# Stick-breaking attention on one core: the weights' transposes moved from TensorE to VectorE's 32x32 blocks and sixteen small copies

## The reference

```
z         = q @ k.T * HEAD_DIM ** -0.5          # 12 heads x 64, causal
earlier   = k_pos < q_pos
log_beta  = log_sigmoid(z)
log_keep  = where(earlier, log_sigmoid(-z), 0)
log_later = cumsum(log_keep, reverse) - log_keep
weights   = where(earlier, exp(log_beta + log_later), 0)
o_A       = weights @ v
...
o = concat(o_A * silu(g_A), o_B * silu(g_B), o_C * silu(g_C)) @ w_out
```

## Time and profile before

| what | value |
|---|---|
| median of 3 runs | 2174.82 us (2173.72 to 2175.7) |
| the profiled execution | 2172.31 us, span 2170.6 us |
| TensorE matmuls, busy | 2112.1 us (97%) |
| VectorE, busy | 1016.4 us (47%) |
| ScalarE, busy | 735.1 us (34%) |
| granted TensorE clock, mean | 0.993 |

### The profile page before, as it was taken

How to read it: one execution, slowest core, us unless ns; L and a number is a source line. 1 busy time by engine, 2 the same in 40 slices (tenths; PEclk the granted TensorE clock), 3 DMA queues, 4 the chain that set the end, 5 groups by cost and what they waited for, 6 DMA issues and landing times.

```text
span 2170.6 us, 31985 instructions
## 1 busy us (share of the span) xinstructions
PE 2112.1 (97%) x13712; PEld 1909.9 (88%) x13712; DVE 1016.4 (47%) x1947; ACT 735.1 (34%) x1280; POOL 9.4 (0%) x28
## 2 busy tenths in 40 slices
PE   5999999999999999999999999999999999999996
PEld 4998988889888898999999999999999978888885
DVE  7446565656656565433334342444334563334224
ACT  6234343443434343322223232333223453222221
POOL 0000000000000000000000000000000000000000
PEclk8999999999999999999999999999999999999998
DMA  6321312222121222213131222222222352336423
GB/s 239 76 71 45 78 37 64 64 55 74 45 65 50 65 65 44 80 40 85 40 84 40 65 64 56 60 54 54 52 66 51 120 172 98 101 105 241 135 83 126
DMA packets 320678, 174.16 MB, mean 80 GB/s; under 512 B 170440, under 2 KB 295128, under 8 KB 318776
## 3 DMA queue, kind: packets, MB, share of 16 engines
q1 hardware_dynamic: 319368, 164.12, 27.2%
q0 software_dynamic: 1168, 7.99, 0.9%
HBM read 139.21 MB, written 36.06 MB: 81 GB/s over the span
## 4 chain that ended last, share of the span: by engine, by line
PE 89%; DVE 7%; ACT 2%; DMA 1%; issue 0%; SPq 0%; DVEq 0%; ACTq 0%
PE ps L792 19%; PE ps L793 18%; PE ps L794 18%; PE ps L989 6%; PE ps L988 6%; PE ps L987 6%; PE ps L877 3%; PE ps L971 3%; PE ps L844 3%; PE ps L942 3%; PE ps L904 2%; PE ps L889 2%; DVE arena L1380 2%; DVE arena L1374 1%; DVE arena L1388 1%; ACT arena L1171 1%
## 5 line engine op out<-in xcount | busy, mean ns | idle before, releaser
L792 PE MATMUL ps<-act_hi,w_hi 128*128 128x352 f32 x2688 | 887.1, 330 | 9.8 <-DVE arena L1315 5.8
L793 PE MATMUL ps<-act_lo,w_hi 128*128 128x352 f32 x2688 | 870.1, 324 | 0.0
L794 PE MATMUL ps<-act_hi,w_lo 128*128 128x352 f32 x2688 | 870.0, 324 | 0.0
L792 PEld LDWEIGHTS ps<-act_hi,w_hi 128*128 128x128 f32 x2688 | 507.5, 189 | 41.5 <-issue 28.6
L793 PEld LDWEIGHTS ps<-act_lo,w_hi 128*128 128x128 f32 x2688 | 507.9, 189 | 0.0
L794 PEld LDWEIGHTS ps<-act_hi,w_lo 128*128 128x128 f32 x2688 | 507.6, 189 | 0.0
L1291 DVE TENSOR_TENSOR w_lo<-w_raw,w_hi 128x512 fp32r<-128x512 f32 x352 | 240.5, 684 | 321.9 <-ACT w_hi L1149 243.8
L987 PE MATMUL ps<-w_hi,act_hi 128*128 128x512 f32 x576 | 226.5, 393 | 5.4 <-DVE w_lo L1291 3.0
L989 PE MATMUL ps<-w_hi,act_lo 128*128 128x512 f32 x576 | 229.0, 398 | 0.0
L988 PE MATMUL ps<-w_lo,act_hi 128*128 128x512 f32 x576 | 228.1, 396 | 0.0
L1073 ACT ACTIVATE w_hi<-w_raw 128x512 fp32r<-128x512 f32 x224 | 138.9, 623 | 143.0 <-DMA w_raw<-in_w_in_dram 143.0
(11 more groups left out here) (122 smaller groups left out, 1684.2 us busy)
## 6 DMA issues: line engine op xcount, KB each, us to landing
w_raw<-in_w_in_dram SPq DMA_DIRECT2D x176, 256.0 KB, 2.9
w_raw<-in_w_out_dram SPq DMA_DIRECT2D x128, 256.0 KB, 3.0
w_raw<-in_w_in_dram SPq DMA_DIRECT2D x96, 128.0 KB, 2.5
arena<-in_x_prompt_dram SPq DMA_DIRECT2D x8, 1024.0 KB, 6.0
out_dram<-arena SPq DMA_DIRECT2D x14, 512.0 KB, 2.8
value_scratch<-arena SPq DMA_DIRECT2D x48, 132.0 KB, 3.4
arena<-value_scratch SPq DMA_DIRECT2D x12, 512.0 KB, 4.2
mixed_scratch<-arena SPq DMA_DIRECT2D x10, 528.0 KB, 4.0
```

The source lines that it names most:

```text
L792: mm(bank(g, GN), wh, ah, start=(k == 0), stop=False)
L793: mm(bank(g, GN), wh, al, start=False, stop=False)
L794: last = mm(bank(g, GN), wl, ah, start=False, stop=(k == KT - 1))
```

## The change

For steps 0 to 8 of A (`by_blocks`) `stick_turn` is gone from TensorE. In its place VectorE turns the whole tile of 128x1024 in blocks of 32x32 into a new buffer `turned` (1024 columns of the arena), and sixteen copies bring block (i, j) of each 128x128 square back to place (j, i) in `stick`: each copy moves 32 partitions x 8 blocks of 32 columns. ScalarE does nine, VectorE seven. The values wait for both (`wt_act`, `wt_dve`). A score set of banks is free once the subtraction has read it (`t_ready`). The sample's step keeps its five small transposes and its copies. `FLIGHT` is 2, so the number of `stick` buffers is as before, and the expression of `gate_at` gives the same ticks as before. The values of the last unit's last two steps are planned 0.2 ticks later. The cached keys, values and the work area lie 96 columns lower in the arena.

```diff
+FLIGHT = 2
+def by_blocks(u, i):
+    return UNITS[u][0] == "a" and A_STEPS[i][0][0] < TT
...
-        return START[u][n] + 7
+        return START[u][n] + 7.2
...
# pe_plan
-            plan += [(START[u][i], "scores", u, i), (turn_at(u, i), "turn", u, i)]
+            plan.append((START[u][i], "scores", u, i))
+            if not by_blocks(u, i):
+                plan.append((turn_at(u, i), "turn", u, i))
# act_plan
+            if by_blocks(u, i):
+                plan.append((s + 5.3, "place_weights", u, i))
+            else:
+                plan.append((w + (0.25 * pace(u, i) if kind == "b" else 0.5), "turned", u, i))
# dve_plan
+                if by_blocks(u, i):
+                    plan += [(s + 4.75, "turn_weights", u, i), (s + 4.76, "place_weights", u, i)]
...
+        stick = [work[:, 1024 * i:1024 * i + 1024] for i in range(FLIGHT)]
+        turned = work[:, 2048:3072]
...
+        def block_of(ap, q, n):
+            return ap[32 * q:32 * q + 32, :].rearrange("p (b n c) -> p b n c", n=4, c=32)[:, :, n, :]
+        MOVES = [(i, j) for i in range(4) for j in range(4)]
+        ACT_MOVES = 9
         def wait_turned(eng, key):
+            if by_blocks(*key):
+                eng.wait_ge(wt_act, part_no(*key))
+                eng.wait_ge(wt_dve, part_no(*key))
+                return
...
             def set_ready(key):
                 for side in SETS[key]:
-                    if SET_USE[key, side] > 1:
-                        pe.wait_ge(set_free[side], SET_USE[key, side] - 1)
+                    last = SET_BEFORE[key, side]
+                    if last is None:
+                        continue
+                    if by_blocks(*last):
+                        pe.wait_ge(t_ready, step_no(*last))
+                    else:
+                        pe.wait_ge(set_free[side], SET_FREE[last, side])
...
# ScalarE
+                elif what == "place_weights":
+                    s = stick[(STEP0[u] + n) % FLIGHT]
+                    act.wait_ge(wt_blocks, part_no(u, n))
+                    for i, j in MOVES[:ACT_MOVES]:
+                        last = fn(block_of(s, j, i), block_of(turned, i, j), ACT.Copy)
+                    last.then_inc(wt_act, 1)
# VectorE
+                elif what == "turn_weights":
+                    dve.wait_ge(w_ready, step_no(u, n))
+                    s = stick[(STEP0[u] + n) % FLIGHT]
+                    if part_no(u, n) > 1:
+                        dve.wait_ge(wt_act, part_no(u, n) - 1)
+                        dve.wait_ge(wt_dve, part_no(u, n) - 1)
+                    v.transpose(turned, s).then_inc(wt_blocks, 1)
+                elif what == "place_weights":
+                    s = stick[(STEP0[u] + n) % FLIGHT]
+                    dve.wait_ge(wt_blocks, part_no(u, n))
+                    for i, j in MOVES[ACT_MOVES:]:
+                        last = v.tensor_copy(block_of(s, j, i), block_of(turned, i, j))
+                    last.then_inc(wt_dve, 1)
```

More of the change, by code:

```diff
@@ L157, in values_at @@
     if kind == "a":
[L158 to L162 removed]
+        if n + FLIGHT < STEPS["a"]:
+            return START[u][n + FLIGHT] - 0.02
+        if u < LAST_A:
+            return START[u + 1][n + FLIGHT - STEPS["a"]] - 0.02
+        return START[u][n] + 7.2
     if kind == "c":
@@ L188 @@
     for side in SETS[key]:
-        SET_USE[key, side] = sum(1 for k in SETS if side in SETS[k])
+        users = [k for k in SETS if side in SETS[k]]
+        SET_BEFORE[key, side] = users[-2] if len(users) > 1 else None
+        SET_FREE[key, side] = sum(not by_blocks(*k) for k in users)
 def pe_plan():
@@ L230, in act_plan @@
                 plan.append((s + 0.65 * pace(u, i), "softmax", u, i))
-            plan.append((w + (0.25 * pace(u, i) if kind == "b" else 0.5), "turned", u, i))
+            if by_blocks(u, i):
+                plan.append((s + 5.3, "place_weights", u, i))
+            else:
+                plan.append((w + (0.25 * pace(u, i) if kind == "b" else 0.5), "turned", u, i))
         plan += [(gate_at(u) - 0.7 + 1.2 * n, "gate", u, n) for n in range(3)]
@@ L240, in gate_at @@
 def gate_at(u):
-    return SLOT[u] + 14.0
+    return 12 * TILE_OF["g", u] + 2.0
 def bias_at(u):
@@ L357, in build @@
         k_turned = arena[:, 7584:7584 + TOK]
-        kcT = arena[:, 8736:9248]
-        vc = arena[:, 9248:9760].rearrange("p (b c) -> p b c", b=4)
-        work = arena[:, 9760:13892]
-        stick = [work[:, 1024 * i:1024 * i + 1024] for i in (0, 1)]
+        kcT = arena[:, 8640:9152]
+        vc = arena[:, 9152:9664].rearrange("p (b c) -> p b c", b=4)
+        work = arena[:, 9664:13892]
+        stick = [work[:, 1024 * i:1024 * i + 1024] for i in range(FLIGHT)]
         c_s = stick
+        turned = work[:, 2048:3072]
         c_bias = work[:, 2560:3840].rearrange("p (h c) -> p h c", h=2)
```

63 lines of the change are left out of this document (26 added, 37 removed).

## The result

The changed kernel takes 2239.4 us (median of 4 runs, 2238.28 to 2240.27) against 2175.3 for the kernel before beside it: a ratio of 1.0295 [1.0278, 1.0313]. It is slower by 64 us; forecast were 2186 us, and 2160 to 2224 as the range.

The account below looks back on a forecast made before the run. TensorE was taken to bound the kernel before, the ScalarE-VectorE ring after. A unit: 92.4 + 37.0 = 129.4 us against 127.6, +11 us over six; 2172.3 + 11 = 2183 profiled, 2186 median, range 2160 to 2224.

Parts of the forecast that it names:

- The ring of ScalarE and VectorE: Closed loop in A from one step's maximum to the next: 13.1 us against TensorE's 11.8, setting the pace to step 7.
- the 0.27: Most that each of VectorE's seven block copies in a step of A should cost, in us; 1.9 in all.
- price (b): ScalarE's nine copies of 32 x 256 elements in a step of A: 0.317 us each, 2.85 us in all.
- The upper bound, 0.42: High end for one ScalarE block copy from SBUF, in us, with no overlap between copies.
- the seven steps: Stretch from maximum 0 to maximum 7 of a unit of A, extras included: 92.4 us.
- The forecast's rest of 37.0: Remainder of a unit of A after maximum 7, in us, where TensorE leads again; makes the unit 129.4.
- the stretch led by TensorE: End of each unit of A, after maximum 7, where the sample step is short: 37.0 us.
- my reading of a tick: TensorE's time for one tick of products in A, read from its timeline: 1.95 us.
- The second (same ring, copies at 0.42): Rival: small copies in A cost the full 0.42 us without overlap, giving 2225 us; chance 0.22.
- The first (full gain): Rival: two steps of slack in A hide everything, TensorE keeps its pace, time falls by 55 to 2120; chance 0.08.
- The shares of busy time (60% and 40%): VectorE and ScalarE busy in A before the change, read as neither engine being full.
- "TensorE sets the time": Claim for A before the change: TensorE busy 682.0 of 690 us, the two other engines waiting for it.

Follow-up runs that it names:

- the added transposes: Changed kernel with TensorE also making the 54 x 8 transposes, from the keys, result read by nobody: 2257.54 us, 1.0378 of the kernel before.
- the two experiments on forms: Changed kernel with each unit of A copying blocks in another form (moved or in place, gaps, partitions, changing quarters), values wrong in units 1 to 5: 2196.5 and 2197.3 us.
- the first set of forms: Changed kernel, block copies varied by unit: moved or in place, with or without gaps, 32 or 128 partitions; 2196.5 us in its one run.
- two DMA queues: Changed kernel with twelve blocks placed by DMAs, six each from SyncE and GpSimd, four copied by VectorE, copies out of PSUM 0.15 tick earlier: 2112.90 us.
- the one-line change of the plan: Kernel before the change with only its copies out of PSUM planned 0.15 tick earlier: 2161.51 us, 0.9944 of the kernel before.
- one DMA queue: Changed kernel with the twelve blocks off the diagonal placed by DMAs from SyncE's queue, the four on it copied by VectorE: 2175.75 us.

## Why the prediction was wrong

**What held.** The transposes went, and what was added cost TensorE nothing by itself. The ring of ScalarE and VectorE took the pace: the exp follows the copies without a gap in most steps, TensorE stops at the ends of tiles for some 4 us, three times a unit, and the sum of the ring's steps was built as forecast. Block transpose 1.24 us, all other members of the ring at their prices. VectorE's seven copies took 2.09 us for 1.9: two scalings in 0.62 are 0.31 each, and the 0.27 that I took from that row does not stand in it. TensorE had room that it could not use, as the added transposes show.

**The step that failed** is price (b): nine copies at 0.317 from the overlap of the earlier trace rows. They take 0.427 each. The row was of four instructions on 128 partitions, all on the same ones; that the overlap needs this I could not see in it, and the two experiments on forms showed it. The upper bound, 0.42, was named and right, and had a chance of 0.22: two rows of single instructions stood behind it (1058 and 659 ns), and one row of a series of another kind against it.

The Trainium skill's page "ScalarE: Activation LUTs" (section on what a table load costs) has ACTIVATEs back to back overlap by about 93 ns. The trace agrees for copies that stay on the same partitions (0.11 to 0.12 us) and not for those that change them. The Trainium skill's page "VectorE: DVE Perf Modes", section on the TRN2 errata, gave an estimate of 0.40 for a small copy, paid each time. The measured 0.427 is near it, so of the two pages I had followed the wrong one for this kernel.

**The size.** The correction for copies, 7 x 9 x 0.11 = 6.9 us a unit, makes the seven steps 92.4 + 6.9 = 99.3; measured, as the mean of six units, 99.3. The forecast's rest of 37.0 is 138.1 - 99.3 = 38.8. So in the terms of the sum, of the 8.7 us a unit that were missing, 6.9 are price (b) and 1.8 the stretch led by TensorE. (0.2 of these are my reading of a tick: 7.86 / 4 is 1.97, not 1.95.) Over six units that is 52 us, and 2183 + 52 = 2235 for a profiled time of 2239.

This is how the sum closes; it is not what the right price would have saved. The units whose copies stay on their quarter show less: 5.0 us a unit off ScalarE's copies brought 2.3 and 2.5 us in the first set of forms and 4.4 in the second, against the same units of the changed kernel, 3.1 on average. In that proportion, an estimate, the 6.9 us are worth some 4.2 a unit, 25 us in all, and a kernel with copies at 0.317 would have taken about 2214, not 2186. So about half of the miss lies in the price. The other half is what the sum left out. What fills it is read from waits only: where the ring gets shorter it meets TensorE's late scores (1.47 us in the row shown), and TensorE has stalls and the half clock behind it. How these share it was not measured.

**The clock.** I had written that it should stay at 1.00, and that pauses would cost more than their length if it fell. It fell: 0.974 over the run, 0.95 in A, and 1.2 GHz after each of the 18 stalls of 3.5 to 4.7 us. One of the three of a unit lies in the stretch that TensorE leads: from maximum 7 of the second unit to the next maximum 0 (370.23 to 408.81), and over the same stretch behind three other units, the mean clock is 0.96 for 38.6 us. That is some 1.5 us of full speed lost, an estimate, beside the 1.8 that the sum lacks there. What the clock alone costs was not measured. That it costs little while the ring leads, since TensorE stops again anyway, is only argued.

**The rivals.** The second (same ring, copies at 0.42) was the right one; its 2225 is 14 us short, 11 of them the last 1.8 us a unit. That it came so near is in part luck, since it rests on the same sum. The first (full gain) is what the kernel gives once the copies leave both queues: 2112.9 with two DMA queues, of which some 14 are the earlier copies out of PSUM. The shares of busy time (60% and 40%) spoke for it, and were no evidence: at 76% and 54% the two engines set the pace.

**Not seen in the kernel before.** "TensorE sets the time" was not all: small waits for copies out of PSUM, of which the earlier trace rows shows 5.8 us, held 13.7 us of the whole, as the one-line change of the plan showed. The list of waits has a second line for them, and it counts less than they cost. In the list and in TensorE's timeline of the kernel before:

```profile
PE ps L792 <- DVE arena L1312: 3.4, 6, 0.6
...
314.77 0.40 PE L792 MATMUL ps<-act_hi,w_hi 128*128 128x352 f32 x1 [0.53 <-DVE arena L1315]
```

The list has 0.53 us here, from the modelled end of the matmul before. By the starts, 313.92, 314.77 and then 315.01, two intervals of 0.16 became 0.85 and 0.24: 0.77 us. The three waits of a unit come to 2.3 us in this way, which is what the edit gave (127.6 to 125.3).

**Open.** Why the overlap is lost where the target begins at another quarter, whether a change of the source alone does the same, and whether the restart at half clock decides where stalls come in the ring through TensorE.

## What to carry to other kernels

Read a wait's cost from the starts before and behind it, not from the idle time alone. Price a series of small instructions by a series of the same kind, with the same partitions and the same changes between them; a series of wide ones does not stand for it, and the high bound is the better guess until it is measured. When work leaves the engine that sets the pace, add up the closed ring that the in-order queues form with what is added, and ask of each queue what stands behind the new instructions: here the place of copies of 0.5 us in it was worth 31 us, 14 of them even without the change. Most moves between partitions can leave the compute engines by DMA (twelve of sixteen did here), if their issues are spread over queues so that they land before they are due.

## What the runs showed of the hardware

- Copies of 32x256 follow each other at 0.427 us on ScalarE and 0.30 on VectorE when the quarter of partitions changes from one to the next, and 0.12 and 0.10 us sooner where it stays (nine in 3.11 us with six such transitions, seven in 1.61 with five). 128 partitions cost no more than 32 (three in 1.02 us).
- On ScalarE an exp of 128 partitions overlapped the copy of 32 ahead of it by 0.1 us when that copy's target began at partition 0 as its own did, and started 0.02 us behind its end when it began at another quarter.
- After each idle time of 3.5 to 4.7 us in A of the changed kernel TensorE worked at half its clock for some microseconds (matmuls 0.29 apart for 0.16). With one DMA queue it did so after 2.05 us as well: values at 275.89 were followed by scores of 2.08 us instead of 1.13. In the same run it kept the full clock behind idle times of 2.9 to 3.1 us (at 543.89, 783.52 and 796.71), so the length of the pause alone did not decide.
- Matmuls that read their moving operand in four runs of 32 columns were as fast as with 128 in a row (1.02 us for sixteen).
- With two queues SyncE issued a DMA of 32 KB between SBUF places in about 0.61 us, GpSimd in 0.50 to 0.57; they land 1.8 to 2.0 us after the issue (median).
